# An encoder block with expert lookup on one core: eight places for gathered rows from the first row on, the last two heads' queries inside the second pair, and two reorderings on ScalarE

## What is computed

```
q = (ht @ w_q).reshape(T, PEER_HEADS, 2, half)
s1 = jnp.einsum('thd,hnd->thn', q[:, :, 0], sub_k1); s2 = jnp.einsum('thd,hnd->thn', q[:, :, 1], sub_k2)
v1, i1 = lax.top_k(s1, PEER_TOPK); v2, i2 = lax.top_k(s2, PEER_TOPK)
sc, ci = lax.top_k((v1[..., :, None] + v2[..., None, :]).reshape(...), PEER_TOPK)
eidx = i1[ci // 16] * PEER_KEYS + i2[ci % 16];  gate = softmax(sc)
a = einsum('cd,chkd->chk', h, u_emb[eidx]);  w = gate * gelu(a)
out = einsum('chk,chkd->cd', w, v_emb[eidx])
```

## Time and profile before

| what | value |
|---|---|
| median of 3 runs | 1921.96 us (1919.48 to 1923.14) |
| the profiled execution | 1921.12 us, of which the span is 1919.2 us |
| TensorE (PE) busy | 1749.0 us, 91% |
| VectorE (DVE) busy | 1277.3 us, 67% |
| GpSimd (POOL) busy | 936.5 us, 49% |
| ScalarE (ACT) busy | 524.2 us, 27% |
| moved by DMA | 608.83 MB, mean 317 GB/s |
| mean granted TensorE clock | 0.943 of full |

### The profile page before, as it was taken

The page is one execution under the profiler, slowest core; times in us unless marked ns, Lnnn a source line. Parts: engine busy times, 40 slices in busy tenths (PEclk is TensorE's granted clock), DMA queues, the critical chain, the costliest instruction groups (busy, mean ns, idle before and its releaser), DMA issues.

```text
span 1919.2 us, 32065 instructions
## 1 busy us (share of the span) xinstructions
PE 1749.0 (91%) x12662; PEld 1176.8 (61%) x12662; DVE 1277.3 (67%) x2472; ACT 524.2 (27%) x1005; POOL 936.5 (49%) x712
## 2 busy tenths in 40 slices
PE   6999989999999999989898898987999898989966
PEld 5988878888999888856565565654444232223310
DVE  4536688887455458988687787878999454444521
ACT  6623646555544431122322322232000000000010
POOL 2022223332153004766765566666788675645562
PEclk9999999999999999989999999999556999999987
DMA  4478879998655759999999999999999999999998
GB/s 191 161 172 187 184 164 206 202 211 188 238 177 195 268 193 335 381 403 415 403 411 389 380 396 381 411 398 378 393 366 359 406 411 413 405 412 411 384 382 330
DMA packets 127126, 608.83 MB, mean 317 GB/s; under 512 B 33182, under 2 KB 33182, under 8 KB 62110
## 3 DMA queue, kind: packets, MB, share of 16 engines
q0 software_dynamic: 96768, 435.04, 63.6%
q1 hardware_dynamic: 30224, 171.96, 24.5%
HBM read 759.15 MB, written 2.10 MB: 397 GB/s over the span
## 4 chain that ended last, share of the span: by engine, by line
PE 42%; DMA 32%; DVE 12%; issue 8%; POOL 5%; ACT 1%; POOLq 0%; DVEq 0%; SPq 0%; ACTq 0%
DMA uv<-v_tab,eidT 19%; DMA uv<-u_tab,eid 11%; DVE uv L1741 5%; PE ps L1875 5%; PE ps L2248 4%; PE ps L2216 4%; POOL uv L660 3%; PE ps L1792 3%; PE ps L1793 3%; PE ps L1794 3%; PE ps L1880 2%; POOL uv L679 2%; PE ps L1882 2%; PE ps L1881 2%; PE ps L2292 2%
## 5 line engine op out<-in xcount | busy, mean ns | idle before, releaser
L1741 DVE CUSTOM_DVE_ANT_0 uv<-uv,xn 128x2048 f32<-128x2048 f32 x256 | 585.9, 2293 | 297.2 <-DMA uv<-u_tab,eid 269.5
L679 POOL DMA_INDIRECT uv<-v_tab,eidT x256 | 435.7, 1702 | 182.6 <-PE ps L2216 100.9
L660 POOL DMA_INDIRECT uv<-u_tab,eid x256 | 321.9, 1257 | 351.6 <-DVE av L1741 158.1
L2216 PE MATMUL ps<-uv,late 128*32 128x512 f32 x2048 | 316.8, 697 | 125.9 <-DMA uv<-v_tab,eidT 119.5
L2248 PE MATMUL ps<-h2T,ring 128*128 128x256 f32 x1152 | 279.1, 386 | 0.0
L2248 PEld LDWEIGHTS ps<-h2T,ring 128*128 128x128 f32 x1152 | 212.7, 195 | 26.6 <-issue 2.5
L2216 PEld LDWEIGHTS ps<-uv,late 128*32 128x32 f32 x2048 | 46.3, 115 | 267.0 <-DMA uv<-v_tab,eidT 205.2
L1046 ACT ACTIVATE ring<-ps 128x512 f32<-128x512 f32 x144 | 85.8, 596 | 316.4 <-PE ps L2241 266.9
L1155 DVE TENSOR_TENSOR low_ring<-ring,wh 128x2048 fp32r<-128x2048 f32 x43 | 101.1, 2353 | 74.9 <-ACT wh L714 74.8
L628 POOL DMA_DIRECT2D parts<-W x80 | 70.3, 879 | 152.5 <-ACT parts L832 128.1
L624 POOL DMA_DIRECT2D parts<-W x80 | 47.6, 596 | 170.1 <-PE ps L1882 104.1
(11 more groups left out here) (373 smaller groups left out, 3149.0 us busy)
## 6 DMA issues: line engine op xcount, KB each, us to landing
ring<-W SPq DMA_DIRECT2D x61, 1024.0 KB
parts<-W POOLq DMA_DIRECT2D x160, 320.0 KB, 5.5
ring<-v_tab SPq DMA_DIRECT2D x36, 1024.0 KB
ring<-u_tab SPq DMA_DIRECT2D x34, 1024.0 KB
...
uv<-u_tab,eid POOLq DMA_INDIRECT x256
uv<-v_tab,eidT POOLq DMA_INDIRECT x256
```

Of the source, the lines that this page charges most:

```text
L660: pool.indirect_dma_start(rows_to, None, u_tab, bass.IndirectOffsetOnAxis(ap=eid[:, p, i:i + 1], axis=0), bounds_check=E0 * NK - 1, oob_is ...
L679: pool.indirect_dma_start(rows_to, None, v_tab, bass.IndirectOffsetOnAxis(ap=eidT[:, p, tokens_of(p, r):tokens_of(p, r) + 1], axis=0), bou ...
L1741: nc.vector.tensor_tensor_reduce(rows_in, rows_in, xn[:, T, :], 1.0, 0.0, ALU.mult, ALU.add, av[:, p % 2, i:i + 1]).then_inc(s_dot, 1)
L2216: ins = nc.tensor.matmul(ps[32 * n:32 * n + 32, j, :], zd[:, p % 2, 32 * q:32 * q + 32], rows_in[:, n * 512:(n + 1) * 512], start=(p == 4 ...
```

## The change

1. **Eight places from the first row.** All u rows of pair 0 use eight buffers, so row m waits for dot m-8 throughout (`input_place`, `freed_by`, `V_FIRST`, `U_ALL`). The guard for the scratch of the squares moves to row 5. `PICKS_FROM` goes from 6 to 8: selection steps start two places later.
2. **Root made ahead.** ScalarE loads the square-root table with a dummy root before `square(1)` and runs `root(1)` right behind the square, ahead of the copies.
3. **The last group of queries moves.** The four query tiles and the scores of heads 6 and 7 leave the stretch ahead of the pairs and run in slots 32 to 40: one part of a query tile ahead of each pick of slots 32 to 39, scores in slots 35, 36, 39 and 40.
4. **The dense rounds start at slot 40** instead of 32, and come 13 in 9 slots instead of 4 in 3. `PACK` stays 143.
5. **SyncE's loads.** The first two table tiles are loaded after the 8th and the 10th of the ring loads of this stretch, no longer ahead of them, and the loop is written out.
6. **Scan.** In steps 1 to 3 of the first block ScalarE makes sines and angle tables one step earlier than before: `cos_sin(0, t)` and `turns(0, t+1)` come ahead of the gate halves of step t, and in step 2 `input_rows` comes first.

```diff
@@ -361,7 +361,7 @@
         s_oh, s_g, s_aw, s_dvd = (sem(n) for n in ("s_oh", "s_g", "s_aw", "s_dvd"))
 
         LAG = 2
-        PICKS_FROM = 6
+        PICKS_FROM = 8
         FIRST_HALVES = ((), ((2, 0), (2, 1)), ((3, 0),), ((3, 1),), ((4, 0),), ((4, 1),), ((5, 0),), ((5, 1),))
         FIRST_MINUS = (((2, 0), (2, 1)), ((3, 0), (3, 1)), ((4, 0),), ((4, 1),), ((5, 0),), ((5, 1),), (), ((6, 0), (6, 1)))
         FIRST_OUT = ((0,), (1,), (2,), (), (3,), (), (4,), ())
@@ -400,7 +400,7 @@
 
         def rounds_by(at):
 
-            return min(max(0, 4 * (at - PICKS) // 3), ROUNDS)
+            return min(max(0, 13 * (at - PICKS - 8) // 9), ROUNDS)
 
         def rounds_at(at):
 
@@ -425,21 +425,15 @@
 
         def input_place(m):
 
-            k = m - TOPK
-            if 0 <= k < TOPK and k % TWICE >= UV:
-                return uv[:, m % UV, 1, :], s_vv[m % UV], k // TWICE
-            uses = m // UV if m < TOPK else TOPK // UV + (k // TWICE if m < PICKS else TOPK // TWICE + (m - PICKS) // UV)
+            if m < PICKS and m % TWICE >= UV:
+                return uv[:, m % UV, 1, :], s_vv[m % UV], m // TWICE
+            uses = m // TWICE if m < PICKS else PICKS // TWICE + (m - PICKS) // UV
             return uv[:, m % UV, 0, :], s_u[m % UV], uses
 
         def freed_by(m):
 
-            k = m - TOPK
-            if m < TOPK + UV:
-                return m - UV
-            if m < TOPK + TWICE:
-                return -1
             return m - TWICE if m < PICKS + UV else m - UV
-        V_FIRST, U_ALL = TOPK // TWICE, (PICKS * PAIRS - TOPK // 2) // UV
+        V_FIRST, U_ALL = PICKS // TWICE, (PICKS * PAIRS - PICKS // 2) // UV
 
         FINALS = ((0, slice(0, 4)), (1, slice(0, 3)), (1, slice(3, 4)))
         SQUARED, ROOTED = (4, 8, 10), (5, 9, 11)
@@ -558,16 +552,14 @@
             for s in range(RING):
                 sp.wait_ge(s_wdone, W_PQ + s + 1)
                 sp.dma_start(ring[:, s, :], W[W_PQ + 3 + s, :, :]).then_inc(s_w[s], 16)
-            sp.wait_ge(s_sq2, 1)
-            sp.wait_ge(s_rows, 1)
-            sp.wait_ge(s_wdone, RING + W_PQ + 3)
-            for i in range(2):
-                sp.dma_start(input_tile(i), u_tab[(E0 + i) * NK:(E0 + i + 1) * NK, :]).then_inc(s_third, 16)
-            with sp.Fori(0, 2) as i:
-                for s in range(RING):
-                    sp.wait_ge(s_wdone, W_PQ + 8 + s + RING * i)
-                    sp.dma_start(ring[:, s, :], W[bass.ds(W_PQ + 7 + s + RING * i, 1), :, :].rearrange("a p n -> (a p) n")
-                                 ).then_inc(s_w[s], 16)
+            for n in range(4, 12):
+                sp.wait_ge(s_wdone, W_PQ + n + 4)
+                sp.dma_start(ring[:, n % RING, :], W[W_PQ + n + 3, :, :]).then_inc(s_w[n % RING], 16)
+                if n in (7, 9):
+                    i = (n - 7) // 2
+                    sp.wait_ge(s_sq2, 1)
+                    sp.wait_ge(s_rows, 1)
+                    sp.dma_start(input_tile(i), u_tab[(E0 + i) * NK:(E0 + i + 1) * NK, :]).then_inc(s_third, 16)
             sp.wait_ge(s_wdone, W_PQ + 16)
             sp.dma_start(ring[:, 0, :], W[W_PQ + 15, :, :]).then_inc(s_w[0], 16)
             for i in range(2, XT):
@@ -652,7 +644,7 @@
                     pool.wait_ge(s_rows, TT)
                 if p == 0 and i == 2:
                     pool.wait_ge(s_wdone, RING + W_PQ + 2)
-                if p == 0 and i == TOPK + UV:
+                if p == 0 and i == UV + 1:
                     pool.wait_ge(s_sq2, 1)
                 rows_to, landed, _ = input_place(m)
                 if freed_by(m) >= 0:
@@ -862,18 +854,25 @@
 
             def scan_body(b, first=False, last=False):
                 for t in range(PPL):
-                    if not (first and t == 1):
+                    ahead = first and t < PPC
+                    if not ahead:
                         turns(b, t)
                     if not first:
                         minus_high(*behind(b, t, 1), 0)
-                    if t >= 2 or not first:
+                    if not first or t > PPC:
                         cos_sin(*behind(b, t, 1))
                     if t % PPC == 0 and (t or not first):
                         inputs_high(b, t // PPC)
                     if first and t == 2:
                         input_rows(*after(b, t))
+                    if ahead and t:
+                        cos_sin(b, t)
+                        if t + 1 < PPC:
+                            turns(b, t + 1)
                     if first:
                         for n, (g, half) in enumerate(FIRST_MINUS[t]):
+                            if t == 0 and n == 0:
+                                turns(b, 0)
                             minus_high(b, g, half)
                             if t == 0 and n == 0:
                                 act.wait_ge(s_pt, 2 * HEADS)
@@ -999,12 +998,13 @@
             act.wait_ge(s_nf, 1)
             nc.scalar.activation(sct0[:, :], ps[:, 0, 0:2 * NK], ACT.Copy, scale=st[:, 2:3]).then_inc(s_fq, 1)
             gate_exp(0)
+            nc.scalar.activation(st[:, 14:15], st[:, 15:16], ACT.Sqrt)
             square(1)
+            root(1)
             last_rows_T(1)
             for q in range(2):
                 act.wait_ge(s_wdone, RING + W_PQ + 1 + q)
                 nc.scalar.activation(qp[:, q, P:SEQ], ps[:, 2 + q, P:SEQ], ACT.Copy).then_inc(s_qp, 1)
-            root(1)
             act.wait_ge(s_ps, 1)
             act.wait_ge(s_nf, 2)
             nc.scalar.activation(sct[:, PH, :], ps[:, 6, 2 * NK:4 * NK], ACT.Copy, scale=st[:, 3:4]).then_inc(s_psc, 1)
@@ -1080,17 +1080,15 @@
             peer_query(2, 2)
             peer_scores(0, 2)
             peer_query(3, 2)
-            peer_query(0, 3)
             peer_scores(1, 2)
-            peer_query(1, 3)
-            peer_query(2, 3)
-            peer_scores(0, 3)
-            peer_query(3, 3)
-            peer_scores(1, 3)
             for p in range(1, PAIRS + 1):
                 exps = list(chosen_in(p))
                 for i in range(PICKS):
                     at = PICKS * p + i
+                    if p == 1 and i in (1, 3, 5, 7):
+                        peer_query(i // 2, PH // 2 - 1)
+                    if p == 1 and i in (5, 8):
+                        peer_scores(i // 8, PH // 2 - 1)
                     if i == 0:
                         gelus(p - 1, 1)
                         if p == PAIRS // 2 + 1:
@@ -2306,7 +2304,7 @@
             nc.tensor.matmul(ps[:, 4, SEQ:2 * SEQ], ones, roots_on[:, :, :].rearrange("p t n -> p (t n)"), start=True, stop=True).then_inc(s_tot, 1)
             peer_scores(3, 0)
             pe.wait_ge(s_ag, 1)
-            for g in range(1, PH // 2):
+            for g in range(1, PH // 2 - 1):
                 for q in range(4):
                     for part in range(2):
                         peer_query(q, g, part)
@@ -2314,13 +2312,18 @@
                         peer_scores(3, g - 1)
                     if q:
                         peer_scores(q - 1, g)
-            peer_scores(3, PH // 2 - 1)
-            pe.wait_ge(s_qp, 2 + 16)
-            pe.wait_ge(s_psc, 2 + PH)
+            peer_scores(3, PH // 2 - 2)
             inputs, spread, outputs = dense_inputs(), gates_spread(), dense_outputs()
             for p in range(1, PAIRS + 1):
                 for i in range(PICKS):
                     at = PICKS * p + i
+                    if p == 1 and i < 8:
+                        peer_query(i // 2, PH // 2 - 1, i % 2)
+                    if p == 1 and i in (3, 4, 7, 8):
+                        peer_scores((3, 4, 7, 8).index(i), PH // 2 - 1)
+                    if p == 1 and i == 8:
+                        pe.wait_ge(s_qp, 2 + 16)
+                        pe.wait_ge(s_psc, 2 + PH)
                     for n in rounds_at(at):
                         next(inputs)
                     for _ in range(halves_by(at) - halves_by(at - 1)):

```

## The result

| | before | changed |
|---|---|---|
| median | 1922.35 us (1919.05 to 1925.77, 8 runs) | 1927.88 us (1925.94 to 1930.81, 8 runs) |
| ratio to before | | 1.0028 [1.0018, 1.0038] |
| profiled execution | 1921.12 us | 1929.03 us |
| moved by DMA | 608.83 MB, 317 GB/s | 608.83 MB, 316 GB/s |
| TensorE busy | 1749.0 us | 1744.0 us |

The changed kernel is slower by 0.28%, where the forecast was 0.25% faster. A ratio of 1 lies outside the interval. The same work is done and the same bytes are moved, so the time went into gaps.

The account below looks back on a forecast made before the run. TensorE was taken to hold most of the chain up to about 700 us, full DMA from about 780. Terms -4.5 + 1 - 1.4 = -4.9 took 1921.1 to 1916.2; 0.8 us to the median gave 1917.1, range 1908 to 1928.

Parts of the forecast that it names:

- the scan's 1.4 us: Scan, step 2: VectorE's angle-table wait ends, products start at 221.8 instead of 223.24, a gain of 1.4 us.
- at 809 + 4 = 813: First pick: dot 31 ends at about 809 and the pick starts 4 us later, 14 us earlier than 827.1.
- 0 to 2 us: Row 16, needing the second head's selection: possible delay of 0 to 2 us from selecting later, none taken.
- leave the crowd at 722: Opening rows: the two table tiles no longer load beside dot 5, which had waited 5.04 us.
- 35.8 + 3.4: Slots 32 to 40: 35.8 us of work and waits plus 3.4 us for a slow restart, slot 40 at 852.
- DMA owes table tiles 2 and 3 ... 3.5 us: Behind slot 40: 2 MB of table tiles loaded near 848 instead of 820, charged 3.5 us.
- 1 us for hiccups: Slots 40 to 143: late v rows TensorE can no longer catch up, charged 1 us, ends 0 and 10.
- DMA below 350 GB/s from 815 to 850: Sign around the eight slots: DMA below 350 GB/s from 815 to 850 us, full after it.
- Rival 3: DMA full between 740 and 820 absorbs all: v rows at 820, slot 40 at 859, 1920 to 1924 us; 28%.
- Rival 1: TensorE becomes the bound of slots 40 to 143: 1936 us if all waits stay, half gives 1928; 17%.
- Rival 2: Clock stays low through the eight slots: 35 us of TensorE work take 70, some 1950 us; 5%.
- The absorption behind 249.07: Scan: TensorE's 4.44 us idle behind 249.07 absorbs the shift of the products.

Follow-up runs that it names:

- e11: Changed kernel with queries ahead of the pairs, rounds as before, PICKS_FROM 6 and SyncE's loads as before; 1912.22 us, ratio 0.9956.
- e12: Changed kernel with PICKS_FROM back at 6 and SyncE's loads as before, queries still in the slots; 1924.49 us, ratio 1.0012.
- e4b: Changed kernel with only PICKS_FROM back at 6; 1925.81 us, ratio 1.0023.
- e9: Kernel before with the eight places alone, PICKS_FROM staying 6; 1914.41 us, ratio 0.9966.
- e3b: Changed kernel with the queries ahead of the pairs again and the rounds from slot 32 at 4 in 3; 1918.44 us, ratio 0.9988.
- e1b: Kernel before with the scan part alone; 1919.93 us, ratio 0.9992.
- e6: Changed kernel with the queries ahead of the pairs again, dense rounds still from slot 40 at 13 in 9; 1917.30 us, ratio 0.9975.

## Why the prediction was wrong

In the prediction's own sum slot 40 was to start at 852, with the scan's 1.4 us at 850.6, and the stretch behind it was to take 475 + 3.5 + 1 = 479.5. Measured are 861.2 and 481.7. The two misses, 10.6 and 2.2 us, are the whole way from a forecast of -4.9 to +7.9.

**The step that failed: the first pick "at 809 + 4 = 813".** It came at 822.1. The ten microseconds of VectorE's lead were there (dot 8 ended at 732.6, forecast 733.7), but dot 31 ended at 815.4 and not at 809. I had put "0 to 2 us" on row 16 and "take none": with selection two places later its index came at 758.0, and GpSimd stood 18 us. And I had counted it as harmless to good that the table tiles "leave the crowd at 722": they left a hole there (350 GB/s instead of e11's 413) and came back at 752 and 766 among the rows that were late. Between dot 8 and dot 31 VectorE waits for rows where the working had it "nearly without a hole". With both parts taken back (e12) that wait is gone and dot 31 ends at 811.1; with `PICKS_FROM` alone (e4b) at 813.8. VectorE's waits (us in total, times, longest) in the changed kernel from 732 to 816 and in e12 from 732 to 812:

```profile
DVE uv L1739 <- DMA uv<-u_tab,eid: 8.3, 5, 2.5
```

```profile
DVE uv L1741 <- DMA uv<-u_tab,eid: 1.3, 3, 0.6
```

The "4" was short too. In the changed kernel, e4b and e12 alike the first pick starts 6.6 us after dot 31 and 12.2 us after the issue of its v row (809.86 in the changed kernel), which is the last thing it waits for. e9, without root and scan, even has dot 31 ending at 809.9, and its first pick still starts at 821.8.

That first pick was to pay for the eight slots, which took 6.3 us more than before, 39.1 instead of 32.9, as forecast. It was forecast 14 us earlier and came 5.0 earlier; and e3b, with the queries ahead of the pairs, has it at 821.5 all the same. So in this kernel the move of the queries bought next to nothing in front of the slots.

**The eight slots were right in sum, partly by luck.** 35.8 + 3.4 = 39.2 us were forecast from first pick to slot 40, 39.1 measured. The slow restart was dearer in the forecast (3.4) than in the trace: the first pick took 1.94 instead of 1.06 and the first half tile 4.88 instead of 3.72, 2.0 us. The rest took 37.1 and not 35.8, so two errors of about 1.3 us cancel.

**The term that was mis-sized: "DMA owes table tiles 2 and 3 ... 3.5 us", and 1 us for hiccups.** The stretch behind slot 40 grew by 6.6 us, not 4.5. The count also starts at slot 40 and takes the early arrival there as the profit. In a stretch that DMA bounds, the count to keep is bytes against time, and it runs through the slots ahead of slot 40 as well. The prediction had even written "DMA below 350 GB/s from 815 to 850" as a sign to look for, and did not turn that sign into a price: (404 - 350) x 35 us is already 4.7 us. Measured, it was 2.3 MB behind at 860 us.

**The rivals.** Rival 3 (v rows at 820, slot 40 at 859) is what happened, 822 and 861, but its time of 1920 to 1924 used the same 3.5 us. Rival 1's number, 1928, came true without its mechanism: TensorE stood idle 482.0 - 438.3 = 43.7 us in slots 40 to 143, 50.2 before, and DMA kept share 0.99. TensorE did become the bound, but in the eight slots ahead of that stretch, where no rival looked. Rival 2 did not come: the clock was at its lower level until 826.3 and then full for the rest of the eight slots. (Its "24 - 8" should read 24 + 8, which gives the 1950.)

**Right:** the root's table load hidden; the eight places as a gain (e9: -6.5 us where they stand alone); the scan's mechanism, and 1.8 us in the rows for 1.4, though e1b does not show that they reach the end. The absorption behind 249.07 did not come: TensorE still idles 4.45 us there and the shift stayed.

**The clock.** Windows of the changed kernel around the restart:

```profile
796.00:822.00 26.00, 0.00 (x0) 0.00 (x0) 24.22 (x36) 0.31 (x1) 18.71 (x11) 0.50 0.95 368
822.00:827.00 5.00, 4.94 (x17) 2.79 (x18) 4.83 (x13) 0.00 (x0) 2.19 (x1) 0.57 0.90 379
```

TensorE worked until 792.7 and then not until 822.06; the granted clock was 0.50 (1.2 GHz) from 796 on and full (2.4 GHz) again from 826.3, inside the first half query tile, until its wait in slot 43. The Trainium skill ("TensorE: Matmul & The Clock Gate", section "The HAM clock gate") has the slow level as what idleness brings, and the trace agrees. By its "Loop structure" section the wait between matmuls would be the harm; here it cost 2.0 us beside a loss of 7.9. e6 is granted 0.51 and 0.72 of the clock from 820 to 860 and is faster than before.
